# Norm factors by Ln and Exp on ScalarE instead of a root there and a reciprocal on VectorE, in a two-block transformer kernel

## The reference

```python
def _rmsnorm(x, g):
    xf = x.astype(jnp.float32)
    y = xf * lax.rsqrt(jnp.mean(xf * xf, axis=-1, keepdims=True) + EPS)
    return (y * g.astype(jnp.float32)).astype(x.dtype)
```

## Time and profile before

| | |
|---|---|
| Median of 3 runs | 1124.12 us (1122.91 to 1125.45) |
| The profiled execution | 1122.68 us, its span 1120.8 us |
| PE busy | 1095.0 us, 98% |
| PEld busy | 1047.8 us, 93% |
| DVE busy | 731.4 us, 65% |
| ACT busy | 574.3 us, 51% |
| POOL busy | 449.3 us, 40% |

### The profile page before, as it was taken

One profiled execution on the slowest core, in us unless ns is written; L12 is line 12 of the kernel. 1 busy time (PEld: TensorE's weight loads), 2 busy tenths in 40 slices (PEclk: granted clock), 3 DMA queues, 4 the chain that ended last, 5 costly groups with the idle time before them and its releaser, 6 DMA issues.

```text
span 1120.8 us, 23476 instructions
## 1 busy us (share of the span) xinstructions
PE 1095.0 (98%) x9175; PEld 1047.8 (93%) x9175; DVE 731.4 (65%) x1029; ACT 574.3 (51%) x827; POOL 449.3 (40%) x430
## 2 busy tenths in 40 slices
PE   7999999999999989999999999999999999999998
PEld 6896699999999869999999999999998989999997
DVE  5886747777556866877746574457747668777543
ACT  5546745544443664555445447645446445544333
POOL 4465714666302661666622112213533014666300
PEclk9999999999999999999999999999999999999999
DMA  9740147766554425676655454243334445766552
GB/s 294 238 151 1 40 136 205 199 184 184 186 181 158 147 69 157 176 192 184 182 163 192 151 188 142 87 150 113 115 113 149 153 114 155 200 181 183 187 180 77
DMA packets 226408, 175.40 MB, mean 156 GB/s; under 512 B 8720, under 2 KB 207632, under 8 KB 226208
## 3 DMA queue, kind: packets, MB, share of 16 engines
q1 hardware_dynamic: 225056, 173.00, 51.2%
q10 hardware_dynamic: 1248, 1.35, 0.4%
q0 software_dynamic: 32, 0.03, 0.0%
HBM read 173.32 MB, written 1.05 MB: 156 GB/s over the span
## 4 chain that ended last, share of the span: by engine, by line
PE 80%; ACT 6%; DVE 6%; issue 4%; POOL 3%; DMA 0%; DVEq 0%; SPq 0%; POOLq 0%; ACTq 0%
PE psum L629 24%; PE psum L635 24%; PE psum L630 23%; ACT work L1533 2%; ACT w_h L1389 1%; PE psum L1234 1%; POOL work L2733 1%; DVE w_l L1848 1%; DVE work L2045 1%; POOL work L2735 1%; PE psum L675 1%; PE psum L1066 1%; PE psum L1321 1%; PE psum L785 1%; PE psum L681 1%
## 5 line engine op out<-in xcount | busy, mean ns | idle before, releaser
L629 PE MATMUL psum<-xh,w_h 128*128 128x256 f32 (+3 forms) x1760 | 437.7, 286 | 9.5 <-ACT w_h L1454 7.4
L630 PE MATMUL psum<-xl,w_h 128*128 128x256 f32 (+3 forms) x1760 | 431.7, 283 | 0.0
L629 PEld LDWEIGHTS psum<-xh,w_h 128*128 128x128 f32 (+1 forms) x1760 | 331.0, 188 | 15.2 <-ACT w_h L1454 7.4
L630 PEld LDWEIGHTS psum<-xl,w_h 128*128 128x128 f32 (+1 forms) x1760 | 331.8, 189 | 0.5
L1848 DVE TENSOR_TENSOR w_l<-raw,w_h 128x2048 fp32r<-128x2048 f32 (+2 forms) x91 | 202.7, 2227 | 140.3 <-ACT w_h L1389 140.3
L1389 ACT ACTIVATE w_h<-raw 128x2048 fp32r<-128x2048 f32 x92 | 167.7, 1823 | 199.0 <-PE psum L635 190.9
L635 PE MATMUL psum<-xh,w_l 128*128 128x256 f32 (+3 forms) x1760 | 246.6, 283 | 0.7 <-DVE w_l L1848 0.7
L635 PEld LDWEIGHTS psum<-xh,w_l 128*128 128x128 f32 (+1 forms) x1760 | 225.4, 189 | 1.9 <-DVE w_l L1848 1.1
L2630 POOL TENSOR_TENSOR work<-work 128x256 f32<-128x256 f32 x66 | 160.6, 2434 | 136.4 <-ACT work L1587 136.4
L2167 DVE TENSOR_TENSOR w_l<-raw,w_h 128x2048 fp32r<-128x2048 f32 x66 | 151.4, 2293 | 13.9 <-ACT w_h L1574 13.4
L629 PE MATMUL psum<-hid_h,w_h 128*128 128x256 f32 (+1 forms) x592 | 148.4, 282 | 0.5 <-issue 0.5
(11 more groups left out here) (329 smaller groups left out, 1412.6 us busy)
## 6 DMA issues: line engine op xcount, KB each, us to landing
raw<-in_ffn_w_gu SPq DMA_DIRECT2D x88, 512.0 KB, 4.9
raw<-in_w_in SPq DMA_DIRECT2D x26, 1024.0 KB, 5.0
raw<-in_ffn_w_down SPq DMA_DIRECT2D x40, 512.0 KB, 4.5
raw<-in_w_ffn_up SPq DMA_DIRECT2D x22, 512.0 KB, 3.9
raw<-in_w_ffn_gate SPq DMA_DIRECT2D x22, 512.0 KB, 5.1
raw<-in_w_ffn_down SPq DMA_DIRECT2D x20, 512.0 KB, 4.4
raw<-in_nsa_w_in SPq DMA_DIRECT2D x9, 1024.0 KB, 5.7
raw<-in_swa_w_qkv SPq DMA_DIRECT2D x5, 1024.0 KB, 5.3
```

Of the source, the lines that this page charges most:

```text
L629: mm(dst, parts[0][:, k, cols], high, start=first, stop=False)
L630: mm(dst, parts[0][:, k, cols], low, start=False, stop=False)
```

## The change

Each root with its reciprocal becomes `exp(-0.5 * ln(total + eps))`, both on ACT; `s45` becomes `exp(0.5 * ln(...))`. DVE's reciprocals go, and its waits for the factor stay. The preload uses Ln, except ahead of the last norm, which keeps root and reciprocal. PE's filler goes from 19 matmuls to 15, and the conversion of slab `M_GLO + 9` goes from ahead of the squares of norm 7 to behind the last of them.

```diff
-            keep_busy(4, 19)
+            keep_busy(4, 15)
...
-            fn(scrap[:, :], eps_col[:, 0:1], ACT.Sqrt)
+            fn(scrap[:, :], eps_col[:, 0:1], ACT.Ln)
...
-            def preload_root():
+            def preload_root(by=ACT.Ln):
 
-                fn(scrap[:, :], eps_col[:, 0:1], ACT.Sqrt)
+                fn(scrap[:, :], eps_col[:, 0:1], by)
+
+            def inverse_root(dst, logs, total, eps, signal, scale=1.0):
+
+                line.put(fn(logs, total, ACT.Ln, scale=scale, bias=eps))
+                line.settle()
+                line.put(fn(dst, logs, ACT.Exp, scale=-0.5), signal)
...
-                    line.put(fn(root[:, t0:T], bank[6][:, t0:T], ACT.Sqrt, scale=float(D // 32), bias=eps_col[:, 0:1]), root_ready)
+                    inverse_root(rstd[:, t0:T], root[:, t0:T], bank[6][:, t0:T], eps_col[:, 0:1], root_ready, float(D // 32))
                 else:
-                    line.put(fn(root[:, t0:T], bank[7][:, t0:T], ACT.Sqrt, bias=eps_col[:, 0:1]), root_ready)
+                    inverse_root(rstd[:, t0:T], root[:, t0:T], bank[7][:, t0:T], eps_col[:, 0:1], root_ready)
...
-            line.put(fn(s45[:, :], s45[:, :], ACT.Sqrt, bias=eps_col[:, 0:1]))
+            line.put(fn(s45[:, :], s45[:, :], ACT.Ln, bias=eps_col[:, 0:1]))
+            line.settle()
+            line.put(fn(s45[:, :], s45[:, :], ACT.Exp, scale=0.5))
             act.wait_ge(meta_ss, 1)
-            line.put(fn(meta_rstd[:, :], bank[6][:, 0:META], ACT.Sqrt, bias=eps_col[:, 0:1]), meta_root)
+            inverse_root(meta_rstd[:, :], meta_rstd[:, :], bank[6][:, 0:META], eps_col[:, 0:1], meta_root)
             high(5)
...
-                    line.put(fn(root[:, META:T2], bank[7][:, T1:2 * T1], ACT.Sqrt, bias=eps2_col[:, 0:1]), root_ready)
-                    line.put(fn(rstd4, bank[7][:, 0:T1], ACT.Sqrt, bias=eps_col[:, 0:1]), root_ready)
+                    inverse_root(rstd[:, META:T2], root[:, META:T2], bank[7][:, T1:2 * T1], eps2_col[:, 0:1], root_ready)
+                    inverse_root(rstd4, rstd4, bank[7][:, 0:T1], eps_col[:, 0:1], root_ready)
...
-            line.put(fn(go_rs[:, LEAD:T2], bank[6][:, LEAD:T2], ACT.Sqrt, scale=float(D // 256) / D / D, bias=eps3_col[:, 0:1]), go_root)
+            inverse_root(go_rs[:, LEAD:T2], go_rs[:, LEAD:T2], bank[6][:, LEAD:T2], eps3_col[:, 0:1], go_inverse, float(D // 256) / D / D)
             high(M_IN2 + 28)
...
-            high(M_GLO + 9)
-            squares(7, T2, h2, lambda c: (h2_odd if c % 2 else h2_even, c // 2 + 1), t0=LEAD)
+            squares(7, T2, h2, lambda c: (h2_odd if c % 2 else h2_even, c // 2 + 1), lambda c: high(M_GLO + 9) if c == 7 else None, t0=LEAD)
...
                 dve.wait_ge(root_ready, i + 1)
-                line.put(V.reciprocal(rstd[:, t0:T], root[:, t0:T]))
-                line.settle()
```

More of the change, by code:

```diff
@@ L327, in build @@
         g_dist, g_decay, g_qk, g_first, g_att, g_sel = map(sem, ("g_dist", "g_decay", "g_qk", "g_first", "g_att", "g_sel"))
-        go_done, go_taken, go_sq, go_ss, go_root, go_inverse, go_spread, go_ready = map(sem, (
-            "go_done", "go_taken", "go_sq", "go_ss", "go_root", "go_inverse", "go_spread", "go_ready"))
+        go_done, go_taken, go_sq, go_ss, go_inverse, go_spread, go_ready = map(sem, (
+            "go_done", "go_taken", "go_sq", "go_ss", "go_inverse", "go_spread", "go_ready"))
         gate_ready, mix_full, mix_high, mix_ready, z_high, go_full, go_high = map(sem, (
@@ L1609, in down_last @@
                     if c == 4:
-                        preload_root()
+                        preload_root(ACT.Sqrt)
                     act.wait_ge(proj_taken, N_FFN[l] + 44 + c + 1)
@@ L1660, in down_into @@
                     act.wait_ge(ss_step, SS_AT[4] + 10)
-                    line.put(fn(root[:, META:T2], bank[7][:, T1:2 * T1], ACT.Sqrt, bias=eps2_col[:, 0:1]), root_ready)
-                    line.put(fn(rstd4, bank[7][:, 0:T1], ACT.Sqrt, bias=eps_col[:, 0:1]), root_ready)
+                    inverse_root(rstd[:, META:T2], root[:, META:T2], bank[7][:, T1:2 * T1], eps2_col[:, 0:1], root_ready)
+                    inverse_root(rstd4, rstd4, bank[7][:, 0:T1], eps_col[:, 0:1], root_ready)
                 else:
                     act.wait_ge(ss_step, SS_AT[2] + 5)
-                    line.put(fn(root[:, 0:T1], bank[7][:, 0:T1], ACT.Sqrt, bias=eps_col[:, 0:1]), root_ready)
+                    inverse_root(rstd[:, 0:T1], root[:, 0:T1], bank[7][:, 0:T1], eps_col[:, 0:1], root_ready)
             act.dma_start(late_in, A["late_c"]).then_inc(late_loaded, 16)
@@ L1964, in nsa_extra @@
                     dve.wait_ge(meta_root, 1)
-                    line.put(V.reciprocal(meta_rstd[:, :], meta_rstd[:, :]))
                 if i == 12:
@@ L2286, in _ @@
             dve.wait_ge(root_ready, 5)
-            line.put(V.reciprocal(rstd[:, META:T2], root[:, META:T2]))
             line.put(V.tensor_copy(rstd[:, 0:META], meta_rstd[:, :]))
@@ L2311, in take2 @@
                         dve.wait_ge(root_ready, 6)
-                        line.put(V.reciprocal(rstd4, rstd4))
-                        line.settle()
                     if 4 <= c < 12:
@@ L2469, in go_scale @@
                     line.put(V.tensor_tensor(g_o[:, o, LEAD:T2], bank[2 + o // 2][:, LEAD:T2], g_o[:, o, LEAD:T2], ALU.mult), go_full)
-            dve.wait_ge(go_root, 1)
-            line.put(V.reciprocal(go_rs[:, LEAD:T2], go_rs[:, LEAD:T2]), go_inverse)
             dve.wait_ge(gate_ready, 2)
```

## The result

Four executions of each kernel, by their medians: 1133.73 us (1132.57 to 1133.86) against 1123.98 us (1122.91 to 1125.45), a ratio of 1.0084 with a 95% interval of 1.0072 to 1.0096. The direction was forecast (slower, 0.86), the size was not: 1129.6 us with a range up to 1132.5. The profiled execution took 1133.86 us (span 1132.0), 11.18 us more than the profiled one of before.

A forecast was written before the change was run, and what follows sets the result against it. PE was taken as the bound, at full clock, so only its waits counted: 0.2 + 2.95 + 0 - 0.93 + 2.25 + 0.25 - 0.06 + 0.8 = +5.5 us, giving a median of 1129.6 us; range 1126.0 to 1132.5.

The forecast's parts named there:

- The price of a pair: Every Ln and Exp pair: a 1.28 us load between them, another ahead of Ln after an Exp; 49 loads in all.
- place 1: First norm: ACT converts slab 2 later, so DVE starts its low part late; +0.2 us, bounds 0 and 0.25.
- Place 2: s45 and meta_rstd: four loads hold ACT ahead of slab 5, PE waits; +2.95 us, bounds 2.3 and 4.8.
- Place 4: Norm 2, ahead of window attention: without the reciprocal the slab comes sooner; -0.93 us, bounds -1.0 and 0.
- Place 5: Norms 4 and 5: three loads delay the slab behind them; +2.25 us, bounds 1.9 and 3.
- Place 6: Head norm (go_rs): ACT's slab and DVE's low part come later; +0.25 us, bounds 0 and 0.4.
- Norm 7: Last norm: the residual copy PE waits for comes behind Ln, load and Exp; +0.8 us, bounds 0.5 and 0.9.
- Norm 6: Factor on PE's path: -0.06 us; later first square counted 0, bound +0.4; four fewer fillers only lengthen idle time.
- One table: Rival: no load between Ln and Exp anywhere, so factors come 1.35 us sooner; -3.0 us, 1121.1 us; chance 0.06.
- Hidden delays: Rival: PE slack hides ACT's delays at s45/meta_rstd and norms 4 and 5; +0.3 us, 1124.4 us; chance 0.06.
- Late slabs on top: Rival: late low parts release buffers late, so next slabs land late too; +1.8 us, 1131.4 us; chance 0.09.
- Factor path alone: Rival: ACT's queue is overrated, only norm 2 and norm 6 count; -1.0 us, 1123.1 us; chance 0.02.

The follow-up runs named there:

- e2: Kernel before with only s45 and meta_rstd changed to Ln and Exp; 1129.61 us, ratio 1.0048 to the kernel before.
- e7: Kernel before with Ln and Exp for norm 2 alone; 1124.21 us, ratio 1.0002 to the kernel before.
- e6: Kernel before with Ln and Exp for norms 4 and 5 alone; 1127.68 us, ratio 1.0036 to the kernel before.
- e8: Changed kernel with the first residual copy at norm 7 run ahead of the Ln; 1131.93 us, ratio 1.0074 to the kernel before.
- e9: Changed kernel with s45, meta_rstd and norms 4 and 5 back to root and reciprocal; 1125.14 us, ratio 1.0023 to the kernel before.
- e5: Kernel before with three plain 128x2048 copies on ACT ahead of the s45 root, no added table load; 1130.41 us, ratio 1.0058 to the kernel before.
- e4: Changed kernel with preloads replaced by explicit loads of the table set holding Ln and Exp; 1121.14 us, ratio 0.9978 to the kernel before.
- e10: Changed kernel run again, unedited; 1133.81 us, ratio 1.0088 to the kernel before.
- e1: Changed kernel with s45 and meta_rstd back to roots and reciprocal; 1127.45 us, ratio 1.0031 to the kernel before.
- e11: Changed kernel with s45, meta_rstd, norms 4 and 5 undone and 24 fillers instead of 15 behind norm 6; 1125.33 us, ratio 1.0012 to the kernel before.
- e3: Changed kernel with 15 filler matmuls in PE's wait ahead of chunk 10; 1131.60 us, ratio 1.0060 to the kernel before.

## Why the prediction was right in the waits and wrong in the time

**The price of a pair.** "I therefore count one load inside every `inverse_root`, and one ahead of its Ln wherever the last function was an Exp": shown, 49 loads, 1.283 us on average in every group, the neighbours in the rows shown within 0.03 us. The Exp of 256 columns took 0.42 (0.40 was taken).

**Places.** Start and place 1 together cost 0.27, just above the bound of 0.25, and the 0.67 at norm 0 itself are partly a lead from the start that is lost again. Place 2 cost 2.68 in the changed kernel, 2.7 alone (e2), and 3.1 where the clock did not fall behind it. Place 4 gave 1.10, and 1.09 alone (e7); its bound was 1.0. Place 5 cost 2.42, and 2.41 alone (e6). Place 6 cost 0.37, within its bound of 0.4. Norm 7 cost 0.93, just above its bound of 0.9, and all of it goes with the copy moved (e8). Single errors of up to 0.3 cancel: that the sum is 5.5 against 5.5 is partly luck.

**Norm 6 and the fillers.** "Four filler matmuls less only lengthen that idle time" may be wrong in its "only": the idle time grew from 0.80 to 1.77 us, and in e8 and e9 the clock fell behind it. The changed kernel's own profile has 1.77 us of idle there too, without a fall, and of the seven profiles with 0.81 us or less none has one.

**The step that failed** is the first: "at a granted clock of 1.00 for the whole span. So PE is the bound, and only what makes PE wait longer or shorter counts." PE's speed was taken as given, and the sum has no term for it. The reading was too coarse as well: the column rounds 0.998, and it shows nothing of the first 12 us, in which the matmuls stand 0.21 us apart. The runs showed in its place that the same matmuls can run for 3.4 us at 1.2 GHz: four such stretches in the profile of the changed kernel and none among the matmuls of the kernel before, worth 1.4 to 1.5 us each, 5.9 us in all. The one near 50 is tied to the wait ahead of it (four profiles of five with the wait, none of eight without it; copies in place of loads do the same, e5). The three others stand at spots where kernels without that wait fall too. In medians: the waits' 5.5, and a mean clock lower by 0.0047 (0.9926 over eight executions against 0.9973 over the 64 of before) at 0.9 us for each 0.001 (4.2 us), are 9.7 us; measured were 9.75.

**The rivals.** One table: the mechanism did not hold for the changed kernel, but e4 came out near the time worked out for it (1121.14 against 1121.1; 3.4 us under its own "before" where 3.0 were forecast). Hidden delays: refuted by PE's waits of 2.61 and 1.85 us. Late slabs on top: behind the wait at 48.77 PE waits for a slab only once more for over 0.25 us, the 1.85 us at 651.77. Factor path alone: refuted by the same waits.

**Left open.** What decides the other falls was not settled. Of thirteen profiles seven have one near 72 to 80 (the changed kernel, e10, e2, and without the wait at 46 to 49 e1, e4, e7, e11), four near 396 to 405 (the changed kernel, e10, e3, e4), seven near 751 to 763 (the changed kernel, e10, e3, e6, e7, e8, e11). The profile of before has none, yet in about half of its executions (34 of 64 at 0.997 or less) the mean clock says that there are one or two. Behind the wait of 1.85 us at norms 4 and 5 none of the six profiles that have it shows a fall at once. And every edited kernel has a lower mean clock than the "before" beside it, e4 and e7 too, which have no long wait of PE (by 0.0015 and 0.0010): about a third of the clock that the changed kernel loses may have nothing to do with its long waits.

## What to carry to other kernels

When an edit moves work to an engine that feeds TensorE, price what is queued behind it there. In this kernel each table load held ACT 1.28 us, and Ln and Exp shared one only where the program itself loaded the set that has both; the trace shows it by the loads that stand between them. A wait of TensorE can cost more than itself: allow in the range for a stretch at half clock behind it. Here one followed the wait of 2.6 us in four profiles of five, idle time of 1.77 us in two of six and that of 1.85 us in none of six, and cost 1.1 to 1.6 us. Filling the wait with matmuls may help; e3 and e11 point that way without showing it. Where times spread by 0.2% from one execution to the next, compare executions at equal mean clock before a difference of that size is given a cause.

## What was unexpected of the hardware

- Every stretch of lower clock seen between the first and the last matmuls, behind the first 12 us, lasted 3.4 us and was at exactly half. Such stretches came with idle times of 1.77 us (e8, e9) and of 2.6 to 2.7 us (the changed kernel, e10, e2, e5), and also behind matmuls of 30 columns with no long wait. The same idle times came without a fall too: 2.62 us in e8, 1.77 us at norm 6 and 1.85 us at 651.77 in the changed kernel.
- Falls stand at a few spots of the program and come back there in kernels with different edits, in some profiles and not in others.
- The kernel before takes 1122.2 to 1122.8 us at a mean clock of 0.999 and 1124.5 to 1126.0 at 0.996, with nothing changed.
